# First group of each feed-forward pass in a new order of products, in a two-layer hybrid encoder kernel on one Trainium2 core

## What is computed

```python
def rmsnorm(x, g):
    xf = x * lax.rsqrt(jnp.mean(x * x, axis=-1, keepdims=True) + EPS)
    return xf * g
def swiglu(h, w_gate, w_up, w_down):
    return (jax.nn.silu(h @ w_gate) * (h @ w_up)) @ w_down
for layer in range(2):
    h = h + 0.5 * swiglu(rmsnorm(h, g[0]), ...)
    h = h + (even_mixer if layer % 2 == 0 else odd_mixer)(rmsnorm(h, g[1]), ...)
    h = h + 0.5 * swiglu(rmsnorm(h, g[2]), ...)
return rmsnorm(h, final_norm)[:, N_META:]
```

## Time and profile before

| | |
|---|---|
| median of three runs | 1894.08 us |
| profiled execution | 1894.9 us |
| its span, first to last instruction | 1893.1 us |
| PE busy | 1834.6 us (97%) |
| DVE busy | 1356.6 us (72%) |
| ACT busy | 868.6 us (46%) |
| mean granted TensorE clock | 0.989 of full |

### The profile page before, as it was taken

How to read it: one execution, slowest core, us unless ns; L and a number is a source line. 1 busy time by engine, 2 the same in 40 slices (tenths; PEclk the granted TensorE clock), 3 DMA queues, 4 the chain that set the end, 5 groups by cost and what they waited for, 6 DMA issues and landing times.

```text
span 1893.1 us, 31889 instructions
## 1 busy us (share of the span) xinstructions
PE 1834.6 (97%) x13095; PEld 1726.3 (91%) x13095; DVE 1356.6 (72%) x1798; ACT 868.6 (46%) x1368; POOL 53.2 (3%) x68
## 2 busy tenths in 40 slices
PE   8799999999998999999989999999999989999997
PEld 8799999999998999999979999998998879889986
DVE  7866876657777866886778678766656778668855
ACT  6443554334445543554455435544423455435542
POOL 0000000000000000000000000000123000000000
PEclk9899999999999999999999999999999999999999
DMA  7123223331222233223222323233212123333231
GB/s 187 69 87 114 90 92 103 118 122 66 68 68 73 95 95 106 90 101 101 78 78 101 98 93 101 93 114 115 79 67 68 67 68 101 97 104 101 94 113 61
DMA packets 81495, 176.81 MB, mean 93 GB/s; under 512 B 7172, under 2 KB 12580, under 8 KB 81352
## 3 DMA queue, kind: packets, MB, share of 16 engines
q1 hardware_dynamic: 80936, 174.49, 28.8%
q10 hardware_dynamic: 416, 0.29, 0.0%
HBM read 171.35 MB, written 3.41 MB: 92 GB/s over the span
## 4 chain that ended last, share of the span: by engine, by line
PE 85%; DVE 9%; ACT 3%; issue 2%; DMA 0%; SPq 0%; DVEq 0%; ACTq 0%
PE psum L1771 18%; PE psum L1830 12%; PE psum L1832 12%; PE psum L1833 12%; PE psum L1872 8%; PE psum L1781 6%; PE psum L1779 3%; PE psum L1780 3%; PE psum L1784 3%; PE psum L1783 3%; DVE rms L1196 1%; DVE wl L1062 1%; ACT fh L596 1%; DVE fl L1178 1%; ACT wh L534 1%
## 5 line engine op out<-in xcount | busy, mean ns | idle before, releaser
L1830 PE MATMUL psum<-fh,wh 128*128 128x264 f32 (+1 forms) x2016 | 590.3, 293 | 35.8 <-DVE fl L1162 19.9
L1832 PE MATMUL psum<-fl,wh 128*128 128x264 f32 (+1 forms) x2016 | 573.3, 284 | 0.0
L1833 PE MATMUL psum<-fh,wl 128*128 128x264 f32 (+1 forms) x2016 | 573.0, 284 | 0.0
L1830 PEld LDWEIGHTS psum<-fh,wh 128*128 128x128 f32 x2016 | 382.7, 190 | 41.9 <-DVE fl L1162 21.0
L1832 PEld LDWEIGHTS psum<-fl,wh 128*128 128x128 f32 x2016 | 382.2, 190 | 2.7
L1833 PEld LDWEIGHTS psum<-fh,wl 128*128 128x128 f32 x2016 | 382.1, 190 | 0.0
L1062 DVE TENSOR_TENSOR wl<-raw,wh 128x1024 fp32r<-128x1024 f32 x189 | 233.2, 1240 | 152.4 <-ACT wh L534 152.3
L534 ACT ACTIVATE wh<-raw 128x1024 fp32r<-128x1024 f32 x190 | 199.5, 1055 | 273.7 <-PE psum L1771 160.2
L1771 PE MATMUL psum<-xs,wh 128*128 128x264 f32 (+1 forms) x1120 | 204.5, 301 | 4.6 <-DVE xs L1149 3.4
L1781 PE MATMUL psum<-hs,wh 128*128 128x512 f32 x528 | 208.3, 395 | 0.0
L1771 PE MATMUL psum<-hs,wh 128*128 128x512 f32 (+2 forms) x760 | 192.5, 349 | 0.8 <-DVE hs L1281 0.8
(11 more groups left out here) (303 smaller groups left out, 2861.0 us busy)
## 6 DMA issues: line engine op xcount, KB each, us to landing
raw<-in_w_gate_up SPq DMA_DIRECT2D x175, 512.0 KB, 3.6
raw<-in_w_down SPq DMA_DIRECT2D x64, 384.0 KB, 3.2
raw<-in_w_down SPq DMA_DIRECT2D x64, 320.0 KB, 2.9
raw<-in_od_in SPq DMA_DIRECT2D x21, 512.0 KB, 3.5
raw<-in_ev_in SPq DMA_DIRECT2D x18, 512.0 KB, 3.5
raw<-in_ev_out SPq DMA_DIRECT2D x8, 512.0 KB, 3.5
raw<-in_od_out SPq DMA_DIRECT2D x8, 512.0 KB, 3.4
x<-in_x_t SPq DMA_DIRECT2D x8, 264.0 KB, 5.0
```

The source lines that it names most:

```text
L1830: pe.matmul(psum[:, bank, 0:w], wh[:, slot, cols], high_x, start=start and j == 0, stop=False, skip_group_check=True)
L1832: pe.matmul(psum[:, bank, 0:w], wh[:, slot, cols], low_x, start=False, stop=False, skip_group_check=True)
L1833: last = pe.matmul(psum[:, bank, 0:w], wl[:, slot, cols], high_x, start=False, stop=j == 3, skip_group_check=True)
```

## The change

The first group of each pass issues its products in another order: p1 and p5 of both pairs, then p2 of both, then p7 and p6 of both, then p3 and p4 of the first pair. For this p5 starts its own PSUM bank instead of adding to a copy of p1 + p6, so `u_copy` goes in the first groups, and DVE gets one subtraction more per pair (in `c22`). In first groups s1 and s3 change places. The sums over the squares are taken from unsplit float32 (`pair_sums`), into two banks that p7 uses next, so that p7 waits for `root_ready`; before, it was the second p7 that did. The forms of x are made in two steps: B11 and T1 first, then B22, T3, T2 and T4. The weight sums and roundings ahead of a pass are spread over three tiles. ACT loads its function tables earlier, by a tiny activation (`warm`). The start of the program is ordered anew on ACT and DVE. No DMA is added or removed; the slot of a21 is freed by `s3_low` in first groups.

```diff
 # tensor engine, first group of a pass
                     if g == first:
                         p1(n, real, new)
-                        if q == 3 and p == 0:
-                            fresh(n + 1, 2)
-                            pe.matmul(psum[:, 5, 0:BACK], wh[:, 4, 0:P], fh[:, 0, 0, 0:BACK], start=True, stop=True)
+                        p5(n, real, new)
                         p1(n + 1, real, new)
+                        p5(n + 1, real, new)
+                        p2(n, real, new)
+                        p2(n + 1, real, new)
+                        if q and not p:
+                            pair_sums(V_FFN[q], real)
                         p7(n, real, new)
                         p6(n, real, new)
-                        if q and not p:
-                            pe.wait_ge(acc_free, tiles_before(TILE[down_name(q, p)], 3))
-                            sums(V_FFN[q], 3, real)
-                        p2(n, real)
-                        p5(n, real)
-                        if q and not p:
-                            pe.wait_ge(root_ready, V_FFN[q] + 1)
-                        p7(n + 1, real)
+                        p7(n + 1, real, new)
+                        p6(n + 1, real, new)
                         p3(n, real)
-                        p6(n + 1, real)
                         p4(n, real)
-                        p2(n + 1, real)
-                        p5(n + 1, real)
                         continue
...
+            def pair_sums(v, real):
+                t = TILE[down_name(PASS_OF_V[v], 0)]
+                pe.wait_ge(acc_free, tiles_before(t, 1))
+                pe.wait_ge(acc_free, tiles_before(t, 3))
+                pe.wait_ge(ss_ready, KT * (v + 1))
+                lo, w = (N_META, BACK) if real else (0, HALF)
+                for h in range(2):
+                    last = pe.matmul(psum[:, 4 * h + 3, 0:w], ones[:, :], ss[:, lo + w * h:lo + w * (h + 1)], start=True, stop=True)
+                last.then_inc(stat_done, 1)
 # vector engine, forms of x
+            def first_low(q, j, real):
+                w = width(real)
+                dve.wait_ge(first_high, 4 * q + j + 1)
+                dve.wait_ge(t1_negative, 4 * q + j + 1)
+                dve.tensor_tensor(fl[:, B11:T1 + 1:2, j, 0:w], ff[:, B11:T1 + 1:2, j, 0:w], f32(fh[:, 0:2, j, 0:w]),
+                                  ALU.subtract).then_inc(first_ready, 1)
 # vector engine, c22 in a leading group
+                    dve.tensor_tensor(bank, bank, u, ALU.subtract).then_inc(u_added, 1)
+                    dve.wait_ge(u_added, added)
 # scalar engine, forms of x
+            def first_forms(q, j, real):
+                w = width(real)
+                act.wait_ge(t1_ready, 4 * q + j + 1)
+                act.activation(fh[:, 0:2, j, 0:w], ff[:, B11:T1 + 1:2, j, 0:w], ACT.Copy).then_inc(first_high, 1)
+                act.activation(ff[:, T2, j, 0:w], ff[:, T1, j, 0:w], ACT.Copy, scale=-1.0).then_inc(t1_negative, 1)
 # vector engine, down projection (scalar engine alike)
                     if ring_next or i < 6:
                         next_low(n + 2 * i)
+                        if g is not None and i == 5:
+                            low_a11(g)
                         next_low(n + 2 * i + 1)
                     elif i == 6 and g is not None:
                         sum_s1(g)
+                        sum_s3(g)
                         sum_s2(g)
+                        low_s1(g)
+                    elif i == 7 and g is not None:
+                        low_s2(g)
                         low_s3(g)
-                        low_s2(g)
-                    elif i == 7 and g is not None:
                         sum_s4(g)
+                        low_s4(g)
```

More of the change, by code:

```diff
@@ L80, in raw_slot, with leads, leading, ring_place @@
     return (CHUNK[down_name(*PASS_OF[g])] + QUARTERS.index(kind)) % RING
-def form_slot(kind, g):
-    if kind in RING_FORMS:
-        return (CHUNK[down_name(*PASS_OF[g])] + RING_FORMS.index(kind)) % RING
-    return 4 if kind == "a11" else 5
+def leads(g):
+    return g == GROUP[PASS_OF[g]][0]
+def leading(g):
+    return sum(leads(h) for h in range(g + 1))
+def ring_place(kind, g):
+    return RING_FORMS.index("s1" if leads(g) and kind == "s3" else kind)
+def form_slot(kind, g):
+    if kind == "a11":
+        return 4
+    if kind == ("s1" if leads(g) else "s3"):
+        return 5
+    return (CHUNK[down_name(*PASS_OF[g])] + ring_place(kind, g)) % RING
 RAW_COUNT, RAW_BEFORE = {}, {}
@@ L612, in root, with pair_root @@
                                bias=eps_sb[:, 0:1]).then_inc(root_ready, 1)
+            def pair_root(v, real):
+                act.wait_ge(stat_done, v + 1)
+                act.activation(halves(rms, real), psum[:, 3:8:4, 0:width(real)], ACT.Sqrt, scale=1.0 / D_MODEL,
+                               bias=eps_sb[:, 0:1]).then_inc(root_ready, 1)
             def p1_copy(n, real):
@@ L662, in groups @@
                     p1_copy(2 * g, real)
+                    if g == first:
+                        if q and not p:
+                            other_forms(q, 3, real)
+                        p1_copy(2 * g + 1, real)
+                        if (q, p) == (0, 0):
+                            high_s4(g)
+                        high_a22(g)
+                        if q and not p:
+                            pair_root(V_FFN[q], real)
+                            warm(ACT.Silu)
+                        high_a11(g + 1)
                     if g > first:
                         hidden_high(g - 1, real, 0)
-                    u_copy(2 * g, real)
-                    if g == first and q and not p:
-                        root(V_FFN[q], real)
-                    if g > first:
+                        u_copy(2 * g, real)
                         high_s4(g)
@@ L796, in _, with std_rest @@
             high_sum(0)
-            for f in range(STD_F):
-                if f < 2:
-                    high(2 * f + 4)
-                if f == 0:
-                    root(0)
-                if f < 2:
-                    high(2 * f + 5)
-                if f == 2:
-                    act.wait_ge(table_out, 16)
-                    high_a11(0)
-                    high_s3(0)
+            def std_rest(c):
+                act.wait_ge(chunk_done, c + 1)
+                act.activation(spare[:, 1 + c % 2, 0:BACK], back(c % 4, 1), ACT.Copy).then_inc(std_back, 1)
@@ L820, in _ @@
-                if f == 3:
-                    high_s4(0)
-                    high_a22(0)
+            for m in ORDER[0:3]:
+                gained(0, m, False)
+            first_forms(0, 0, False)
+            first_forms(0, 1, False)
+            high(4)
+            for m in ORDER[3:6]:
+                gained(0, m, False)
+            first_forms(0, 2, False)
+            high(5)
+            root(0)
+            std_rest(0)
+            std_silu(0)
+            std_rest(1)
+            std_hidden(0)
@@ new lines, in _ @@
+            high(6)
+            for m in ORDER[6:8]:
+                gained(0, m, False)
+            first_forms(0, 3, False)
+            std_rest(2)
+            std_silu(1)
+            std_rest(3)
+            high(7)
+            std_hidden(1)
+            act.wait_ge(table_out, 16)
+            high_a11(0)
+            high_s1(0)
+            std_rest(4)
+            std_silu(2)
+            other_forms(0, 0, False)
+            std_rest(5)
+            high_s2(0)
+            std_hidden(2)
```

374 lines of the change are left out of this document (209 added, 165 removed).

## The result

The changed kernel took 1906.8 us (median of four runs, 1903.5 to 1907.7) beside 1894.2 for the kernel before on the same chip: ratio 1.0063, 95% interval 1.0046 to 1.0081. It is slower by 12.6 us, where the prediction said +1.3 and ended its range at 1901. The profiled execution took 1907.66 us with a span of 1905.9.

What follows compares the result with a forecast made beforehand. PE bounds the kernel, busy 1834.6 of 1893.1 us. Start +1.1, blocks -3.1, -1.0, -3.2, passes b +7.6, less 0.1 for a matmul: +1.3, so a median of 1895.4 us, range 1888.5 to 1901.

Steps and rivals of the forecast that it cites:

- The starts' waits: Starts of pass a: PE waits 6 us in third block, 1.8 and 2.2 in second, 1.9 and 2.2 in fourth.
- the third block: Pass a: second-group p7 begins 2.9 us earlier, less 1.9 for a clock drop behind the 6 us wait; net -1.0 us.
- The wait for c21: New PE wait in first groups, second-group p7 waiting for DVE's read of p4: 2.0 us, eight times.
- The failed step: Second and fourth block, pass a: zero clock loss counted, as no wait exceeds 2.2 us and 1.68 brought no drop.
- the passes b: Four passes b: no old wait to remove, a new 2.0 us wait between p4 and p7; cost 4 x 1.9 = 7.6 us.
- the start: Program start: second-group p7 at 91.3 us, before 92.1, with one clock loss of 1.9; net +1.1 us.
- The clock rival: Slower: the clock falls at the second and fourth block too, 1.9 us twice, giving 1899.2 us; chance 0.17.
- the prediction's own sign of being wrong: A granted clock under 0.8 around 585 and 1535 us in the profile, adding 2 us each.
- The second block: Pass a: second-group p7 at about 599.0 us, before 602.1; gain 3.1 us, no clock loss.
- The fourth: Fourth block, pass a: second-group p7 at about 1547.5 us, before 1550.7; gain 3.2 us, no clock loss.
- The late root: First root on ACT at 33.7 us, before 26.58; chunk 3 idles 5.7, absorbed. Rival, not absorbed: 1901.1 us, chance 0.13.
- The table load's drain: Rival: ACT's table load also costs its drain, 1.4 us at three starts, giving 1899.6 us; chance 0.04.

## Why the prediction was wrong

*The starts' waits.* Predicted 6 us in the third block (5.42), 5.7 for chunk 3 (5.67), 1 for the root (0.99), and 1.8 and 2.2 in the second (1.72 and 2.09). These are right, and L1162's and L1178's 35 us became 17.4 where 19 was said. In the fourth block 1.9 and 2.2 were said, and PE waited 2.67 us and then not at all. In the third block p2 lost 2.2 us to the clock (5.95 for 3.80), near the 1.9 counted.

*The wait for c21.* Predicted eight times near 2.0 us; measured 14.9 / 8 = 1.86. Right in mechanism, place and size. The chain of the earlier trace rows, 4.57 us, was found again as 4.58.

*The failed step: "I count no clock loss, since no wait exceeds 2.2 us, and a wait of 1.68 us at 945.72 was not followed by a drop."* It was said of two blocks, and the same zero stands silently behind 4 x 1.9 in the passes b and behind the start. In the second block it held: the waits were 1.72, 2.09, 0.99 and 1.85 us, and the clock stayed at 1.00. The single row was right as a row, too: waits of 1.66 to 1.70 us brought no drop in any of eight places, in the two runs made for it. But it was 0.2 us away from the wait for c21, which is 1.85 to 1.90 us long, and behind six of these eight the clock fell. The six take 10.3 us, where the forecast of 1895.4 missed 11.4. They stand where the table is off: in the passes b (+5.5), the third block (+2.3) and the start (+1.6). Their number is chance in part: over all traces waits of 1.84 to 1.90 us brought a drop in 27 of 45 cases.

*The clock rival* named the right mechanism and, for the most part, the wrong places. It put the drops at the second and fourth block and gave them 3.8 us. In the second none came. In the fourth one came behind the wait of 2.67 us, as the prediction's own sign of being wrong had it (a clock under 0.8 around 1535 us; the window from 1534 shows 0.54), and cost next to nothing, as shown below. Behind c21 none came in either, and the rival never priced the passes b, where the same wait stood four times. A drop at all eight, at its own 1.9, would have given 1895.4 + 15.2 = 1910.6, and at six 1906.8. The Trainium skill, TensorE: Matmul & The Clock Gate, section HAM oscillation — how this bites in real kernels, was taken to speak for this rival: a kernel in which each idle stretch leads to a start at the low clock. But its idle stretches are waits for a DMA of about 3 to 5 us, so it says nothing of waits of 2 us. The traces agree with it for waits of 3.3 us and over (45 of 45). Below that a drop comes behind some and not behind others, and hardly ever at 1.73 us and under (1 of 22).

*The second block* is the step that stays off with no drop in it: -3.1 predicted, -1.2 measured. Of its 1.9 us, 0.8 are lost between the pass b and the first wait at 581.48, in which I found no wait that before does not have. Another 0.6 is the walk from p2 to p7 behind the root, 3.4 + 0.8 + 0.9 = 5.1 us in the prediction and 594.26 - 588.59 = 5.67 on the timeline. The rest, 0.5, stays open. It was not tried alone.

*The fourth* came out at -3.4 for -3.2, and that was luck in part. Of the 3.4 us, 2.2 had been won before its first wait, 1.4 of them in the second mixer (1333.67 - 1322.11 = 11.56 us behind the wait at its start, 1364.64 - 1354.53 = 10.11 at the next wait), where before has a low stretch behind a wait of 2.54 us and the changed kernel, with the same wait, has none (1.00 in the 5 us behind it):

```profile
1322.00:1327.00 5.00, 4.89 (x17) 4.09 (x18) 1.38 (x3) 1.70 (x2) 0.00 (x0) 0.67 0.15 51
```

The walk had no such term. And the low clock around 1535, which it did not have either, cost little because the slower matmuls filled the wait for p1's copy that was to come: from the end of the wait of 2.67 us to the p7 behind c21 are 1559.23 - 1534.24 = 24.99 us, and in the run with the root early, with the clock at 1.00 and p2 waiting 2.17 us, 1560.53 - 1535.86 = 24.67.

*The late root.* Predicted as absorbed. The start was 1.6 us worse than said, and the window behind 93.08 holds 1.7 us of low clock. With DVE's three operations early, the second group's first p2 of the program stood at 96.44 us on PE's timeline, 1.4 ahead of before (97.79 there). The late root cost nothing that the trace shows. (The operations listed ahead of it add up to 7.4 us, not the 7.3 of the prediction; the wait came out right all the same.)

*The table load's drain.* The root's place was taken by a tiny activation behind the load (957.52 + 1.28, the next at 958.81): 0.01 us, again no drain.

What the change did right shows once its waits are gone: the second group's p2 of the fourth block stands at 1545.49 us with the early operations in pass a, at 1556.25 before. With its waits taken away the new order is some 10 us faster than the kernel before (1.4 us of it, in the traces, are the mixer's low stretch above), and the waits with the low clock behind them cost 22.

## What to carry to other kernels

Price a new wait of TensorE with its length and, separately, with the low clock behind it; take the second from several rows at that length, since one row without a drop does not show that none comes, and count it at every place where the wait stands. A drop right ahead of another wait can vanish in it. When a reader on another engine comes late, look for idle time of that engine ahead of the chain: work moved there is gone from the path, while work that only changes place within the chain moves the wait one product on. If a wait can't be shortened, a repeated product whose bank starts anew can fill it: here that kept the clock up at no cost in time.

## What the runs showed of the hardware

- How often the granted clock fell behind a wait of PE of a given length (mean clock under 0.95 in the 5.00 us from the end of the wait; all fourteen traces, without the first 16 us and the last 22 us of the program):

| wait, us | where | drops |
|---|---|---|
| 1.66 to 1.73 | forms of x, c21 | 1 of 22 |
| 1.84 to 1.90 | c21 and c22 | 27 of 45 |
| 2.05 to 2.17 | p1's copy, once c21 | 1 of 12 |
| 2.54 | mixer | 6 of 14 |
| 2.67 | form of x, fourth block | 7 of 11 |
| 2.8 to 3.1 | forms of x, only with the old order | 3 of 5 |
| 3.3 and over | starts of a pass a and of the program | 45 of 45 |

- So the length alone is no rule. At one and the same place 0.2 us can decide (0 of 8 against 8 of 9 in the runs made for it), but waits of 2.05 to 2.17 us elsewhere brought fewer drops than those of 1.84 to 1.90, and the wait of 2.54 us, the same in every kernel, had one in some traces and none in others. What else decides was not tried.
- A stretch at the low clock behind a wait for c21 took 1.7 us each time (4.0 x 0.43 or 5.0 x 0.34), nearly as much as the wait itself. The one of 7.00 x 0.46 = 3.2 us at 1534 cost only 0.3 us in the end, since a wait of 2.2 us that was to follow was filled by it.
- Filling 1.46 of 1.86 us with repeated matmuls kept the clock at 1.00 in eight of eight windows.
